# Norms of the first attention by one-pass products of two-part squares, with Newton steps on VectorE

## The chip, the cores and the metric

One core of a Trainium2 chip runs one launch of one program. The metric is the device time of that launch in microseconds, the median of several runs. TensorE does matrix products and transposes into PSUM, VectorE and ScalarE do elementwise work, GpSimd some small work, and SyncE issues most transfers. The engines run in order and meet only at semaphores.

## The reference

Two blocks on x of 512 tokens by 1024. The first is a state-space mixer, a gated feed-forward, a differential attention and a second feed-forward; the second is an mLSTM beside a sparse attention. The change touches the attention of the first block alone:

```python
def rms_norm(x, g):
    return x * rsqrt(mean(x * x, axis=-1) + 1e-6) * g

k = rms_norm(k.reshape(s, 8, 2, 64), k_norm_g)       # 8 heads, two halves of 64
q = rms_norm(q.reshape(s, 8, 2, 64), q_norm_g)
p = softmax(q @ k.T * 64 ** -0.5 + bias, causal)     # one for each half
o = (p[half 0] - lam * p[half 1]) @ v                # 128 wide for each head
o = rms_norm(o, subln_g) * (1 - lam_init)
return o @ out_w
```

## The kernel before

Everything is kept with features on the 128 partitions and the 512 tokens in the free dimension. The large products are made from float32 in three parts: a high part of the weights (ScalarE, L314, float32r) times a high and a low part of the input (L290, L291), and a low part of the weights (VectorE, L325) times the high part (L294). These are one-pass products. Products of plain float32 (scores, transposes, product with v, sums of squares) take two passes. A cell is a 128-row slice of a projection, three one-pass products of 512 columns; a tile is 8 cells (6 or 2 in the output projection).

The first attention works through 8 heads in 3 rounds each; round 0 has query blocks 0 and 1, round 1 block 2, round 2 block 3. I write a round as (h, r). All order is written out by hand in one function for each engine:

- TensorE (`attention_pe`, L671) does, in each round, the 8 cells of a projection tile of the next head (`cells_of`), the scores, then `head_sums(h+1, 0)` in round 0 or `out_sums(h-1)` in round 2, the turn of the previous round's attention (`turn_attn`, L745), the product with v of the round before that (`attn_v`, L756), and in round 1 `head_sums(h+1, 1)`. The last two heads have no new tile to fill rounds with; part of head 7's v tile and the cells of the output projection (`out_cells`) are spread there.
- VectorE (`attention_dve`, L1054) does `combine` of the previous round (L1103 to L1109), `logits` (L1093), the evacuation of the new tile (`evac`, L1066) and the low part of the weights (L325), and the norms' last multiplication (`k_norm` L1074, `q_norm` L1079, `out_norm` L1114).
- ScalarE (`attention_act`, L853) splits the weights, copies the turned attention (`turned`, L906), does the exponentials (`exps`, L898) and the squares (L871), copies and squares a head's output (`head_out`, L913, L914), and starts the inverse roots.

A norm before goes: squares on ScalarE; on TensorE four products that put the squares as the stationary operand and two columns (or one) of ones as the moving one (L699, L767), which gives sums by token in 8 (or 4) columns; mean, Ln and Exp(-0.5 ln) on ScalarE (L875 to L877) on those few columns; one Newton step on GpSimd (`attention_pool`, L1007), which for k and q also spreads the result over 512 columns (L1023); four transposes on TensorE (L709, L717) that turn it to features by tokens in PSUM; and the last multiplication on VectorE.

Of the kernel before, what the change touches and what calls it, by code (L numbers as in the profile page):

```python
# [13 lines left out]
T = 512  # L14
P = 128
# [70 lines left out]
def three_parts(nc, A, out):  # L86
    ctx = ExitStack()
    with ctx:
# [14 lines left out]
        SQ = sb("squares", [P, 2, T])  # L103
        ACC = sb("square_sums", [P, T])
# [12 lines left out]
        CV = sb("conv_rows", [P, 2, T])  # L117
        EMB = sb("floor", [P, T])
        RDB = sb("reciprocals", [P, T])
# [493 lines left out]
        MEAN, LOGS, ROOT, NEWT = ([at(NT, 2) for _ in range(2)] for _ in range(4))  # L613
        INV = [buf.rearrange("p (c d) -> p c d", d=P) for buf in (EMB, RDB)]
        OMEAN, OLOG, OROOT, ONEWT, ORMS = (at(NT) for _ in range(5))
# [9 lines left out]
        hsq = sem("head_squares_ready")  # L625
        hss = sem("head_square_sum_done")
# [3 lines left out]
        newton_step = sem("newton_step")  # L630
        inv_ready = sem("head_inv_rms_ready")
        oroot_ready = sem("out_inv_rms_first_ready")
        ro_ready = sem("out_inv_rms_ready")
        kb_done = sem("k_inv_rms_spread")
        qb_done = sem("q_inv_rms_spread")
        qn_ready = sem("head_q_ready")
        outb_done = sem("out_inv_rms_spread")
# [33 lines left out]
        def attention_pe(pe):  # L671
# [16 lines left out]
            def head_sums(h, which):  # L688

                pe.wait_ge(hsq, 2 * h + which + 1)  # L690
                if which == 0 and h >= 1:
                    pe.wait_ge(v_ready, h)
                if which == 1 and h >= 3:
                    pe.wait_ge(oh_ready, h - 2)
                if which == 1 and h >= 1:
                    pe.wait_ge(qn_ready, h)
                for c in range(NT):
                    at = 8 * which + 2 * c
                    mm = nc.tensor.matmul(BANK[6 + which][:, at:at + 2], SQ[:, which, c * P:(c + 1) * P],  # L699
                                          const("half_ones")[:, 0:P:64], start=True, stop=True)  # L700
                mm.then_inc(hss, 1)

            def spread_norm(h, which):

                pe.wait_ge(inv_ready, 2 * h + which + 1)
                if which == 1 and h >= 2:
                    pe.wait_ge(oroot_ready, h - 1)
                for c in range(NT):
                    mm = nc.tensor.transpose(BANK[6 + which][:, c * P:(c + 1) * P],  # L709
                                             INV[which][:, c, :], IDENT)  # L710
# [2161 lines left out]
```

## Time and profile before

| | |
|---|---|
| median of 3 runs | 2050.57 us (2049.69 to 2050.99) |
| span of the profiled execution | 2047.5 us |
| first attention | from about 763 to 1035 us of the span |
| one steady head | 27.33 us |

The profiled execution is known by its span alone; the timed runs are about 3 us longer. In a timeline a row is a start, a length, engine, line, operation, tile names and how many instructions were merged; an idle time before it stands in brackets with what ended it. Lengths of neighbouring products overlap, so their cost is read from start to start. The rows the prediction uses stand below.

### The profile page before, as it was taken

How to read it: one execution, taken by the hardware profiler on the slowest of the kernel's cores; microseconds unless marked ns; L12 is line 12 of the kernel's file. 1: busy time of each engine (PE TensorE's matmuls, PEld its weight loads, DVE VectorE, ACT ScalarE, POOL GpSimd, SP SyncE). 2: the span in 40 equal slices, each digit the busy share in tenths (PEclk: the TensorE clock that was granted, in tenths of full speed). 3: DMA queues.
4: the chain of work that ended last, by engine and by line, in shares of the span. 5: the costliest groups of instructions: out<-in, count | busy, mean ns of one | idle time of the engine just before them, and what ended most of it. 6: DMA issues, size and time to landing. Idle time of an engine off the chain costs nothing.

```text
span 2047.5 us, 26858 instructions
## 1 busy us (share of the span) xinstructions
PE 2026.5 (99%) x10268; PEld 1635.1 (80%) x10268; DVE 1424.9 (70%) x2093; ACT 927.6 (45%) x1601; POOL 63.3 (3%) x132
## 2 busy tenths in 40 slices
PE   9999999999999999999999999999999999999998
PEld 7887878788888887787778888888777777777787
DVE  7788898777775446566577777447877867566664
ACT  5577775344443234455454444224443332444531
POOL 0000001000000001222000000000000000000000
PEclk9999999999999999999999999999999999999999
DMA  5322222233232333111132332333222224111132
GB/s 177 121 73 73 72 82 63 93 96 100 92 102 81 99 108 114 52 62 38 56 112 94 94 101 83 101 99 104 83 83 77 78 82 165 53 52 52 52 103 83
DMA packets 56225, 179.46 MB, mean 88 GB/s; under 512 B 6287, under 2 KB 9487, under 8 KB 55992
## 3 DMA queue, kind: packets, MB, share of 16 engines
q1 hardware_dynamic: 52416, 167.80, 26.2%
q10 hardware_dynamic: 3704, 10.30, 1.5%
q8 instruction: 61, 1.00, 0.2%
q14 instruction: 44, 0.36, 0.1%
HBM read 175.95 MB, written 4.74 MB: 88 GB/s over the span
## 4 chain that ended last, share of the span: by engine, by line
PE 50%; DVE 1%; ACT 1%; DMA 0%; issue 0%; DVEq 0%
PE bankpair L290 14%; PE bankpair L294 14%; PE bankpair L291 14%; PE bankpair L1532 1%; PE bankpair L1564 1%; PE bankpair L1544 1%; PE bankpair L1400 1%; PE bankpair L1388 1%; PE bankpair L1476 0%; PE bankpair L526 0%; PE bankpair L1457 0%; DMA weight_ring<-up_dram 0%; PE bankpair L1407 0%; DVE residual L2191 0%; PE bankpair L1560 0%; ACT L1726 0%
## 5 line engine op out<-in xcount | busy, mean ns | idle before, releaser
L290 PE MATMUL bankpair<-scaled_in_high,weights_high 128*128 128x512 f32 x1856 | 743.8, 401 | 1.8 <-DVE scaled_in_low L999 0.7
L291 PE MATMUL bankpair<-scaled_in_low,weights_high 128*128 128x512 f32 x1856 | 723.5, 390 | 0.0
L314 ACT ACTIVATE weights_high<-weight_ring 128x1024 fp32r<-128x1024 f32 (+3 forms) x344 | 334.0, 972 | 339.7 <-DMA weight_ring<-down_dram 148.6
L294 PE MATMUL bankpair<-scaled_in_high,weights_low 128*128 128x512 f32 x1856 | 463.0, 389 | 0.0
L325 DVE TENSOR_TENSOR weights_low<-weight_ring,weights_high 128x1024 fp32r<-128x1024 f32 (+3 forms) x344 | 384.1, 1125 | 57.4 <-ACT weights_high L314 47.8
L290 PEld LDWEIGHTS bankpair<-scaled_in_high,weights_high 128*128 128x128 f32 x1856 | 348.7, 188 | 83.0 <-issue 6.5
L291 PEld LDWEIGHTS bankpair<-scaled_in_low,weights_high 128*128 128x128 f32 x1856 | 348.8, 188 | 75.5 <-issue 5.7
L294 PEld LDWEIGHTS bankpair<-scaled_in_high,weights_low 128*128 128x128 f32 x1856 | 348.4, 188 | 72.5
L290 PE MATMUL bankpair<-gated_high,weights_high 128*128 128x512 f32 x448 | 175.1, 391 | 1.9 <-DVE gated_low L2629 1.2
L291 PE MATMUL bankpair<-gated_low,weights_high 128*128 128x512 f32 x384 | 149.4, 389 | 0.0
L589 DVE SCALAR_TENSOR_TENSOR conv_rows<-padded_rows,params,conv_rows 128x512 f32<-128x512 f32 x176 | 131.8, 749 | 7.0 <-ACT conv_rows L558 3.8
L583 DVE TENSOR_TENSOR padded_rows<-bankpair,inv_rms 128x512 f32<-128x512 f32 x88 | 60.9, 691 | 106.4 <-PE bankpair L294 106.1
L558 ACT ACTIVATE conv_rows<-padded_rows,params 128x512 f32<-128x512 f32 x88 | 71.9, 817 | 121.3 <-DVE padded_rows L583 120.8
L294 PE MATMUL bankpair<-gated_high,weights_low 128*128 128x512 f32 x448 | 115.2, 389 | 0.0
L290 PEld LDWEIGHTS bankpair<-gated_high,weights_high 128*128 128x128 f32 x448 | 84.1, 188 | 21.2 <-DVE gated_low L2629 2.5
L294 PEld LDWEIGHTS bankpair<-gated_high,weights_low 128*128 128x128 f32 x448 | 84.1, 188 | 17.5
L500 DVE TENSOR_TENSOR residual<-residual,bankpair 128x512 f32<-128x512 f32 x24 | 16.5, 687 | 98.9 <-PE bankpair L294 98.7
L291 PEld LDWEIGHTS bankpair<-gated_low,weights_high 128*128 128x128 f32 x384 | 72.1, 188 | 14.8
L1093 DVE CUSTOM_DVE_ANT_0 arena<-bankpair,arena 128x128 f32<-128x128 f32 (+3 forms) x64 | 31.4, 491 | 61.2 <-PE bankpair L735 59.7
L1886 DVE TENSOR_TENSOR padded_rows<-bankpair,inv_rms 128x512 f32<-128x512 f32 x44 | 30.4, 690 | 48.4 <-PE bankpair L294 47.2
L566 ACT ACTIVATE gated_high<-conv_rows 128x512 fp32r<-128x512 f32 x44 | 27.8, 632 | 73.3 <-DVE conv_rows L594 73.3
L563 ACT ACTIVATE arena<-conv_rows 128x512 f32<-128x512 f32 x44 | 27.8, 633 | 70.8 <-DVE conv_rows L589 70.8
(396 smaller groups left out, 2396.4 us busy)
## 6 DMA issues: line engine op xcount, KB each, us to landing
weight_ring<-up_dram SPq DMA_DIRECT2D x88, 512.0 KB, 3.5
weight_ring<-w_in_dram SPq DMA_DIRECT2D x70, 512.0 KB, 3.5
weight_ring<-in_w_dram SPq DMA_DIRECT2D x40, 512.0 KB, 3.6
weight_ring<-down_dram SPq DMA_DIRECT2D x32, 384.0 KB, 3.1
weight_ring<-kvq_dram SPq DMA_DIRECT2D x24, 512.0 KB, 3.5
weight_ring<-down_dram SPq DMA_DIRECT2D x32, 320.0 KB, 2.8
weight_ring<-out_a_dram SPq DMA_DIRECT2D x8, 512.0 KB, 3.6
weight_ring<-out_b_dram SPq DMA_DIRECT2D x8, 512.0 KB, 3.6
```

Source lines behind the costliest of these rows:

```text
L290: nc.tensor.matmul(bank, WH[:, high_slot, cell], high, start=(k == 0), stop=False)
L291: nc.tensor.matmul(bank, WH[:, high_slot, cell], low, start=False, stop=False)
L294: mm = nc.tensor.matmul(bank, WL[:, slot, cell], high, start=False, stop=(c == last_k))
L314: nc.scalar.activation(WH[:, (PART0[name] + k) % SLOTS, 0:n], RAW[:, b % SLOTS, 0:n], ACT.Copy).then_inc(high_ready, 1)
L325: nc.vector.tensor_tensor(WL[:, b % SLOTS, 0:n], RAW[:, b % SLOTS, 0:n], WH[:, (PART0[name] + k) % SLOTS, 0:n].bitcast(F32), ALU.subtract) ...
L558: nc.scalar.activation(CV[:, b, :], U[:, b, 3:3 + T], ACT.Identity, bias=par(f"ffn_conv{layer}", 4 * n + 3), scale=par(f"ffn_conv{layer}", ...
L563: nc.scalar.activation(GATE, CV[:, 0, :], ACT.Silu).then_inc(row_used, 1)
L566: nc.scalar.activation(FFH[:, m, :], CV[:, 1, :], ACT.Copy).then_inc(gated_high, 1)
L583: fr.step(nc.vector.tensor_tensor(U[:, b, 3:3 + T], gemm_bank(name, n), RS[:, :], ALU.mult))
L589: (step if b or k == 0 else cv).step(nc.vector.scalar_tensor_tensor(CV[:, b, :], U[:, b, 1 + k:1 + k + T], par(f"ffn_conv{layer}", 4 * n + ...
L1093: (lr if last else step).step(nc.vector.tensor_tensor_reduce(PR[w % 2][c][:, at:at + n], BANK[2 + c][:, at:at + n], BIAS[:, h, T - n:T], - ...
L1886: fr.step(nc.vector.tensor_tensor(dst, gemm_bank(W2, n), RS[:, :], ALU.mult))
```

## The change

The norms become: high part of the squares (ScalarE, float32r) and the whole squares (ScalarE), low part (VectorE); on TensorE two accumulating one-pass products of 512 columns with a full 128 by 128 matrix of ones (or of two 64 by 64 blocks of ones) as the stationary operand, so that the sum already stands on every partition; Ln and Exp on ScalarE on 512 columns; one Newton step as three scalar_tensor_tensor on VectorE on 512 columns; and the last multiplication, which now reads SBUF. GpSimd has no part left in it, and the transposes `spread_norm` and `spread_out` are gone. The two matrices of ones are copied to float32r by ScalarE at the start of the attention. Lines with no content but "..." stand for what is left out.

```diff
@@ TensorE
             def head_sums(h, which):
-                pe.wait_ge(hsq, 2 * h + which + 1)
+                pe.wait_ge(hsl, 2 * h + which + 1)
                 if which == 0 and h >= 1:
                     pe.wait_ge(v_ready, h)
+                if which == 1 and h >= 1:
+                    pe.wait_ge(hs_read[1], h)
                 if which == 1 and h >= 3:
-                    pe.wait_ge(oh_ready, h - 2)
-                if which == 1 and h >= 1:
-                    pe.wait_ge(qn_ready, h)
-                for c in range(NT):
-                    at = 8 * which + 2 * c
-                    mm = nc.tensor.matmul(BANK[6 + which][:, at:at + 2], SQ[:, which, c * P:(c + 1) * P],
-                                          const("half_ones")[:, 0:P:64], start=True, stop=True)
-                mm.then_inc(hss, 1)
-            def spread_norm(h, which):
...
-            def spread_out(h):
...
+                    pe.wait_ge(os_read, h - 2)
+                nc.tensor.matmul(BANK[6 + which][:, :], HALF_R, ROOT_R[which], start=True, stop=False)
+                nc.tensor.matmul(BANK[6 + which][:, :], HALF_R, SQ_R[:, which, :], start=False,
+                                 stop=True).then_inc(hss, 1)
             def out_sums(h):
...
+                pe.wait_ge(osl, h + 1)
+                pe.wait_ge(hs_read[1], min(h + 3, AH))
                 if h >= 1:
-                    pe.wait_ge(oh_ready, h)
-                for c in range(NT):
-                    mm = nc.tensor.matmul(BANK[7][:, c:c + 1], SQO[:, c * P:(c + 1) * P], ONES[:, 0:1], start=True, stop=True)
-                mm.then_inc(oss_done, 1)
+                    pe.wait_ge(os_read, h)
+                nc.tensor.matmul(BANK[7][:, :], ONES_R, OUT_R[:, :], start=True, stop=False)
+                nc.tensor.matmul(BANK[7][:, :], ONES_R, ACC_R[:, :], start=False, stop=True).then_inc(oss_done, 1)
...
-            out_cells(33, 36)
+            out_cells(33, 38)
             out_sums(AH - 1)
-            out_cells(36, 42)
-            spread_out(AH - 1)
-            out_cells(42, 48)
+            out_cells(38, 48)
@@ ScalarE
+            act.wait_ge(gemm_done, TILE0["down0"] + KD)
+            nc.scalar.activation(ONES_R, ONES[:, :], ACT.Copy).then_inc(ones_r, 1)
+            nc.scalar.activation(HALF_R, const("half_ones"), ACT.Copy).then_inc(ones_r, 1)
...
-                nc.scalar.activation(SQ[:, which, :], U[:, 0, 3:3 + T] if which == 0 else QN[h % 2],
-                                     ACT.Square).then_inc(hsq, 1)
+                    act.wait_ge((kq_ready, qn_ready)[which], h)
+                raw = U[:, 0, 3:3 + T] if which == 0 else QN[h % 2]
+                nc.scalar.activation(ROOT_R[which], raw, ACT.Square).then_inc(hsq, 1)
+                nc.scalar.activation(SQ[:, which, :], raw, ACT.Square).then_inc(hsq, 1)
...
+            def first_root(root, sums, scale):
+                logs.step(nc.scalar.activation(root, sums, ACT.Ln, bias=EPSC[:, 0:1], scale=scale))
+                return nc.scalar.activation(root, root, ACT.Exp, scale=-0.5)
...
                 nc.scalar.activation(OB, BANK[5][:, :], ACT.Copy).then_inc(ob_ready, 1)
+                nc.scalar.activation(OUT_R[:, :], BANK[5][:, :], ACT.Square).then_inc(ob_ready, 1)
                 nc.scalar.activation(SQO, BANK[5][:, :], ACT.Square).then_inc(ob_ready, 1)
...
                     exps(h, r)
                     if r == 0 and h + 1 < AH:
+                        inverse(h + 1, 0)
                         squares(h + 1, 1)
-                        inverse(h + 1, 0)
@@ GpSimd
-        def attention_pool(pool):
...
@@ VectorE
+            def low_squares(h, which):
+                dve.wait_ge(hsq, 2 * (2 * h + which + 1))
+                sq = SQ[:, which, :]
+                nc.vector.tensor_tensor(SQ_R[:, which, :], sq, ROOT_R[which].bitcast(F32), ALU.subtract).then_inc(hsl, 1)
+            def low_out_squares(h):
+                dve.wait_ge(ob_ready, 3 * h + 3)
+                nc.vector.tensor_tensor(ACC_R[:, :], SQO, OUT_R[:, :].bitcast(F32), ALU.subtract).then_inc(osl, 1)
+            def newton(root, sums, n, read):
+                read.step(nc.vector.scalar_tensor_tensor(NEWT, sums, n * EPS, root, ALU.add, ALU.mult))
+                step.step(nc.vector.scalar_tensor_tensor(NEWT, NEWT, -0.5 / n, root, ALU.mult, ALU.mult))
+                step.step(nc.vector.scalar_tensor_tensor(root, NEWT, 1.5, root, ALU.add, ALU.mult))
+            def head_root(h, which):
+                dve.wait_ge(root_ready, 2 * h + which + 1)
+                newton(ROOT[which], BANK[6 + which][:, :], 64, hr_read[which])
+            def out_root(h):
+                dve.wait_ge(oroot_ready, h + 1)
+                newton(OROOT, BANK[7][:, :], P, or_read)
...
             evac(0, 1)
+            low_squares(0, 0)
             evac(0, 2)
+            head_root(0, 0)
             k_norm(0)
+            low_squares(0, 1)
             for h in range(AH):
                 for r in range(NR):
                     w = NR * h + r
                     if w == 0:
                         evac(1, 0)
+                        low_squares(1, 0)
+                    if r == 0 and 1 <= h < AH - 1:
+                        low_squares(h + 1, 0)
                     if r == 0:
+                        if h == 0:
+                            head_root(0, 1)
                         q_norm(h)
                     if w >= 1:
                         combine((w - 1) // NR, (w - 1) % NR)
-                    if r == 2 and h + 1 < AH:
+                    if r >= 1 and h + 1 < AH:
+                        head_root(h + 1, r - 1)
+                    if r == 1 and h + 1 < AH:
                         k_norm(h + 1)
+                        low_squares(h + 1, 1)
+                    if r == 2 and h >= 1:
+                        low_out_squares(h - 1)
+                    if r == 0 and h >= 2:
+                        out_root(h - 2)
                     logits(h, r)
...
+            out_root(AH - 2)
             out_norm(AH - 2)
             low_out(AH - 2)
+            low_out_squares(AH - 1)
...
             add_part("attn_a", 6)
+            out_root(AH - 1)
             out_norm(AH - 1)
             low_out(AH - 1)
```

## Rows read from the trace of the kernel before

**Rows 1.** The page's busy times: engine, busy us, share of the span, instructions.
```profile
PE 2026.5 (99%) x10268; PEld 1635.1 (80%) x10268; DVE 1424.9 (70%) x2093; ACT 927.6 (45%) x1601; POOL 63.3 (3%) x132
```

**Rows 2.** Busy time by stretches: a steady head, head 6, then head 7's last round onward.
```profile
869.04:896.37 27.33, 27.33 (x159) 21.98 (x158) 16.52 (x39) 13.11 (x36) 5.61 (x12) 1.00 0.19 58
951.04:967.75 16.71, 14.83 (x101) 11.64 (x101) 13.16 (x35) 11.94 (x36) 4.99 (x12) 1.00 0.08 24
...
984.10:1007.00 22.90, 22.90 (x125) 19.08 (x125) 12.97 (x24) 11.00 (x27) 0.80 (x4) 1.00 0.16 55
```

**Rows 3.** Timeline of TensorE in rounds 0 and 1 of a steady head.
```profile
869.89 1.05 PE L699 MATMUL bankpair<-constants,squares 128*128 128x2 f32 x8
870.81 0.63 PE L745 MATMUL bankpair<-constants,arena 128*128 128x128 f32 x4
...
871.95 0.60 PE L717 MATMUL bankpair<-constants,arena 128*128 128x128 f32 x4
872.30 0.47 PE L290 MATMUL bankpair<-scaled_in_high,weights_high 128*128 128x512 f32 x1
872.62 0.39 PE L291 MATMUL bankpair<-scaled_in_low,weights_high 128*128 128x512 f32 x1
...
877.95 0.92 PE L735 MATMUL bankpair<-arena 64*128 64x384 f32 x4
```

**Rows 4.** Timeline of VectorE over one steady head.
```profile
860.86 0.69 DVE L1093 CUSTOM_DVE_ANT_0 arena<-bankpair,arena 128x512 f32<-128x512 f32 x1 [3.37 <-PE bankpair L735]
...
862.33 0.69 DVE L1066 TENSOR_TENSOR padded_rows<-bankpair,inv_rms 128x512 f32<-128x512 f32 x1
...
864.20 0.68 DVE L1079 TENSOR_TENSOR arena<-arena,bankpair 128x512 f32<-128x512 f32 x1
...
865.83 0.75 DVE L1109 SCALAR_TENSOR_TENSOR arena<-arena 128x512 f32<-128x512 f32 x1
870.11 0.29 DVE L1093 CUSTOM_DVE_ANT_0 arena<-bankpair,arena 128x128 f32<-128x128 f32 x1 [3.53 <-PE bankpair L735]
...
879.00 0.56 DVE L1093 CUSTOM_DVE_ANT_0 arena<-bankpair,arena 128x384 f32<-128x384 f32 x1 [2.62 <-PE bankpair L735]
...
882.58 0.17 DVE L1103 RECIPROCAL arena<-arena 128x2 f32<-128x2 f32 x1 [0.42 <-ACT arena L898]
```

**Rows 5.** Timeline of ScalarE in round 2 of a steady head.
```profile
861.74 0.26 ACT L875 ACTIVATE arena<-bankpair,eps_column 128x4 f32<-128x4 f32 x1 [4.94 <-PE bankpair L767]
...
862.38 0.47 ACT L906 ACTIVATE arena<-bankpair 128x384 f32<-128x384 f32 x1
862.75 0.72 ACT L898 ACTIVATE arena<-arena 128x512 f32<-128x512 f32 x1
...
864.17 0.62 ACT L871 ACTIVATE squares<-padded_rows 128x512 f32<-128x512 f32 x1
```

**Rows 6.** Timeline of VectorE: logits (5,2), (6,2), (7,0), then combine (7,1).
```profile
942.86 0.69 DVE L1093 CUSTOM_DVE_ANT_0 arena<-bankpair,arena 128x512 f32<-128x512 f32 x1 [3.36 <-PE bankpair L735]
...
964.19 0.69 DVE L1093 CUSTOM_DVE_ANT_0 arena<-bankpair,arena 128x512 f32<-128x512 f32 x1
...
969.36 0.29 DVE L1093 CUSTOM_DVE_ANT_0 arena<-bankpair,arena 128x128 f32<-128x128 f32 x1
...
985.87 0.17 DVE L1103 RECIPROCAL arena<-arena 128x2 f32<-128x2 f32 x1 [2.83 <-ACT arena L898]
```

**Rows 7.** Timelines of TensorE and of VectorE at the attention's start.
```profile
773.71 0.95 PE L699 MATMUL bankpair<-constants,squares 128*128 128x2 f32 x8
...
790.76 0.93 PE L735 MATMUL bankpair<-arena 64*128 64x128 f32 x8
...
766.58 3.35 DVE L366 RECIPROCAL inv_rms<-rms 128x512 f32<-128x512 f32 x1 [0.31 <-ACT rms L357]
...
775.11 0.69 DVE L1066 TENSOR_TENSOR padded_rows<-bankpair,inv_rms 128x512 f32<-128x512 f32 x1
```

**Rows 8.** Timeline of TensorE: the sum of head 6's output squares.
```profile
985.15 1.05 PE L767 MATMUL bankpair<-ones,square_sums 128*128 128x1 f32 x8
```

More of the change, by code:

```diff
@@ L102, in three_parts @@
         WL = sb("weights_low", [P, SLOTS, CELLS * P], F32R)
-        SQ = sb("squares", [P, 2, T])
-        ACC = sb("square_sums", [P, T])
+        ONES_R = sb("ones_for_parts", [P, P], F32R)[:, :]
+        HALF_R = sb("half_ones_for_parts", [P, P], F32R)[:, :]
+        with ExitStack() as whole_squares:
+            SQ = whole_squares.enter_context(nc.sbuf_tensor("squares", [P, 2, T], F32))
+            ACC = whole_squares.enter_context(nc.sbuf_tensor("square_sums", [P, T], F32))
+        SQ_R = sb("squares_low", [P, 2, T], F32R)
+        ACC_R = sb("out_squares_low", [P, T], F32R)
         RS = sb("inv_rms", [P, T])
@@ L612, in three_parts @@
         SUMS = [at(4) for _ in range(2)]
-        MEAN, LOGS, ROOT, NEWT = ([at(NT, 2) for _ in range(2)] for _ in range(4))
-        INV = [buf.rearrange("p (c d) -> p c d", d=P) for buf in (EMB, RDB)]
-        OMEAN, OLOG, OROOT, ONEWT, ORMS = (at(NT) for _ in range(5))
+        ROOT = [CV[:, 0, :], CV[:, 1, :]]
+        OROOT = RDB[:, :]
+        NEWT = EMB[:, :]
+        ROOT_R = [HIGH_R[:, 0, :], HIGH_R[:, 1, :]]
         LAM = at(72)
@@ L824, in attention_pe @@
                             head_sums(h + 1, 1)
[L825 to L831 removed]
+                        if r == 2 and h < AH - 2:
+                            turn_v(h + 1)
                     if (h, r) == (AH - 1, 0):
@@ L870, in squares @@
                     act.wait_ge(hss, 2 * h + which - 1)
-                nc.scalar.activation(SQ[:, which, :], U[:, 0, 3:3 + T] if which == 0 else QN[h % 2],
-                                     ACT.Square).then_inc(hsq, 1)
-            def first_root(mean, log, root, sums, scale):
-                logs.step(nc.scalar.activation(mean, sums, ACT.Identity, bias=EPSC[:, 0:1], scale=scale))
-                logs.step(nc.scalar.activation(log, mean, ACT.Ln))
-                return nc.scalar.activation(root, log, ACT.Exp, scale=-0.5)
+                    act.wait_ge((kq_ready, qn_ready)[which], h)
[5 more added lines that the diff above has]
+                return nc.scalar.activation(root, root, ACT.Exp, scale=-0.5)
             def inverse(h, which):
                 act.wait_ge(hss, 2 * h + which + 1)
-                if h >= 1:
-                    act.wait_ge(inv_ready, 2 * h + which - 1)
-                sums = BANK[6 + which][:, 8 * which:8 * which + 8].rearrange("p (c n) -> p c n", n=2)
-                first_root(MEAN[which], LOGS[which], ROOT[which], sums, 1.0 / 64).then_inc(root_ready, 1)
+                first_root(ROOT[which], BANK[6 + which][:, :], 1.0 / 64).then_inc(root_ready, 1)
             def v_out(h):
@@ L1056, in attention_dve @@
             qn = Count(dve, qn_ready)
+            hr_read, or_read = [Count(dve, s) for s in hs_read], Count(dve, os_read)
             def evac(h, j):
@@ L1112, in out_norm @@
             def out_norm(h):
-                dve.wait_ge(outb_done, h + 1)
-                ohr.step(nc.vector.scalar_tensor_tensor(OH[:, h, :], OB, LAM[:, 69:70], BANK[7][:, :], ALU.mult, ALU.mult))
+                ohr.step(nc.vector.scalar_tensor_tensor(OH[:, h, :], OB, LAM[:, 69:70], OROOT, ALU.mult, ALU.mult))
             def add_part(name, j):
```

88 lines of the change are left out of this document (16 added, 72 removed).

## The prediction

> **What bounds the kernel now.** First the page's busy shares [rows 1]: TensorE is busy 99% of the span, so the program is a chain of TensorE work. Then busy time by stretches [rows 2]: in a steady head of the first attention (27.33 us) TensorE is busy throughout, VectorE 16.5, ScalarE 13.1 and GpSimd 5.6 us, at a granted clock of 1.00. From head 6 on this changes: little projection work is left to fill the rounds, and in the 16.71 us of head 6 TensorE is busy 14.83 and VectorE 13.16 us. Then the timelines of TensorE, VectorE and ScalarE over one steady head [rows 3 to 5], which give the prices, and VectorE's in heads 5 to 7 [rows 6].
>
> I call a round (h, r). TensorE is in order: cells of the projection, scores, sums, the turn of the round before, its product with v. VectorE is in order too: combine of the round before, logits, evacuation, weight split. Its gaps in a steady head are the bracketed 3.37, 3.53, 2.62 and 0.42 us of [rows 4]: 9.9 us free, 17.4 us occupied.
>
> **TensorE's part.** Start to start, a sum of squares costs 0.92 us (869.89 to 870.81) and a spread of four transposes 0.35 (871.95 to 872.30) [rows 3]. A steady head has three of each: 3.8 us are removed. Added are three pairs of one-pass products of 512 columns. 24 such passes take 5.65 us (872.30 to 877.95), 0.235 each, and the first after two-pass work 0.32, so 0.09 for the change of kind [rows 3]. A pair costs between 0.46 and, if it is no cheaper than what it replaces, 0.92 us; I take 0.55, near the passes' own row: 1.65 a head. TensorE alone would need 27.33 - 3.8 + 1.65 = 25.2 us.
>
> **VectorE's part.** Per head three low parts (a tensor_tensor on 512 columns, 0.68 us by L1079, 0.62 start to start where nothing waits) and three Newton passes of three scalar_tensor_tensor each. One is 0.75 us on 512 columns of SBUF, 0.78 with the wait for itself [rows 4]; with a PSUM operand I take the same, as L1079, which has one, is no dearer than its kind. A pass costs 2.34. Sum 3 x 0.62 + 3 x 2.34 = 8.9 us, so VectorE is occupied 17.4 + 8.9 = 26.3 us: more than TensorE's 25.2. The bound passes to VectorE. GpSimd's 5.6 us vanish; nobody waited for long on them.
>
> **ScalarE's part.** A square is 0.62 us, 0.52 start to start; there are three more. Each root becomes Ln and Exp on 512 columns. No row shows that Ln: it lies between the square's 0.62 and the 0.72 of an Exp with bias and running sum [rows 5]. I take 0.64 + 0.62 + 0.03 = 1.3 us to the result, where three small activations took 0.64 (861.74 to 862.38). ScalarE's total, 13.1 + 3 x 0.52 + 3 x 0.6 = 16.5 us, is no bound, but its order matters. In (h, 2) it does out_inverse, turned, exps, then both squares of the next k. out_inverse waits for out_sums, and that for low_out_squares, which VectorE makes just ahead of the same round's logits. Counted from the start of logits(h, 2): product done at 0.95, Ln and Exp to 2.2, turned 0.37, exps 1.42, two squares 1.14: 5.1. VectorE, after logits 1.47, evacuation and split 1.87 [rows 4], reaches low_squares(h+2, 0) at 3.3. It waits 1.8 us, or 1.5 where out_sums begins with the end of the scores.
>
> **A second wait, on TensorE.** In (h, 1) head_sums(h+1, 1) stands ahead of the next round's cells and needs low_squares(h+1, 1), which VectorE ends 2.34 + 0.77 + 0.62 = 3.7 us after the combine that releases turn_attn; TensorE has 1.3 us of work there. It idles some 2.3 us.
>
> **The steady head after.** From logits(h, 2) = 0, low_squares(h+2, 0) starts at 4.8. Then 0.62, q_norm 0.71, combine 1.70, out_root 2.34, logits 1.60, evacuation and split 1.87, out_norm 0.77, combine 2.02, Newton 2.34, k_norm 0.77, low part 0.62: 15.4 on, at 20.2, low_squares(h+2, 1) is done. TensorE then does the pair with its release (0.8), eight cells (5.65) and the scores up to the next logits (1.28): 27.9. VectorE's own way is 27.7. A head takes 27.9 us against 27.33: +0.55, four times (heads 1 to 5): +2.2.
>
> **Before that.** TensorE summed the first squares at 773.71 [rows 7]; now it waits for evac(0, 1), which starts at 775.11, and a low part, to 776.5: 2.8 us. The second sum waits until VectorE is through evac(0, 2), Newton and k_norm. Counted through with the same prices, the first scores start at 794.4 instead of 790.76 [rows 7]: +3.7. Heads 0 and 1 have the (h, 1) wait too, against the sums and spreads saved: +0.4. At logits(5, 2) the lag is 3.7 + 0.4 + 2.2 = 6.3 us.
>
> **Heads 6 and 7 carry the loss,** as TensorE has no cells there that would cover it. From logits(5, 2) to logits(6, 2) it was 964.19 - 942.86 = 21.3 us [rows 6]. Now: the wait to 4.8, then the steps above to the split of (6, 1), 17.2; exps 0.4, combine 1.50, Newton 2.34, low part 0.62: 26.9, so +5.5. From there to logits(7, 0) it was 5.2 us [rows 6]; now out_inverse, turned and exps put the combine at 4.75, then 1.70 and out_root(5) 2.34: 8.8, so +3.6. The lag is 15.4, and the chain low_out, evac, out_norm(5), high_out, low_out(5), scores(7, 1) carries it over unchanged. In (7, 2) out_sums(6) started at 985.15 [rows 8]; with the lag TensorE gets there at 1000.6. Now it waits until VectorE, after the exps, has combined (7, 1) and made the low part. That combine started at 985.87 [rows 6]: 985.87 + 15.4 + 0.49 (one more square ahead on ScalarE) + 1.50 + 0.62 = 1003.9, so +3.3. Lag 18.7. From there TensorE is busy to the end [rows 2], so the lag is carried, less two spreads and a cheaper sum (-1.1), plus about 1.4 for out_sums(7), moved back two cells but behind low_out_squares(7), and for the last Newton pass ahead of attn_b. **End: +19 us.** The sum stands against the profiled 2047.5 us; the timed runs (median 2050.57) have some 3 us around the span, which the change leaves. 2050.6 + 19 = **2069.5 us**, 0.9% slower.
>
> At nothing I cost the two copies that make the one-pass ones: 2 x 0.3 us on ScalarE ahead of high_query, under VectorE's 3.35 us reciprocal [rows 7]; without that cover, 0.6. The same for inverse moved ahead of squares(h+1, 1): VectorE's combine, 2.02 us, covers the root's 1.3.
>
> **Rivals.** (1) The steady heads lose nothing: the waits of 1.5 and 2.3 us fall into slack that I misjudge, a head takes VectorE's bare 26.3 us (-1.0, five times), and heads 6 and 7 lose 2 less. For it: the two waits hang on orders with little margin. Against: the durations alone give head 6 most of its +5.5 and +3.6. Time: 2069.5 - 2.2 - 5 - 2 = 2060; chance 0.18.
> (2) Faster: TensorE stays the bound in every head, 8 x (3.8 - 1.65) = -17 us, 2033. One mechanism: VectorE's additions fit its free time. It decides if a Newton step costs under 0.78 - (26.3 - 25.2)/9 = 0.66 us, and head 6, where VectorE has 3.6 us free of 16.7 [rows 2], still loses. The 0.75 us of the nearest row speaks against it. Chance 0.08. Between it and (1), within 0.2% (4 us, about what a measurement of this kernel can tell from no change): 0.07.
> (3) TensorE's clock. It stays at 1.00 in every stretch read, though TensorE is idle for 1.9 of the 16.71 us of head 6 [rows 2]. After, I expect idle spells of 4.7 us at out_sums(5), 4.1 at the first out_cells, 3.3 at out_sums(6). If the clock then falls to 1.2 GHz, steps of 0.235 become 0.47 for a while. The first two falls lie under VectorE's lateness, the third does not; it is bounded by nothing and by the seven cells behind it at half speed (5 us): up to +5, 2074. Chance 0.12.
> The Trainium skill ("TensorE: Matmul & The Clock Gate", Part 1) has the clock at 1.2 GHz after an idle spell until work has been sustained again; by that rule (3) is what happens and 2074 the time. No row here has a spell long enough to say.
> My own forecast: 0.55.
>
> **How the numbers follow.** The likeliest case is 2069.5; its own range, from Newton steps 5% cheaper and a pair at 0.46 (-5) to a pair at 0.92, Ln at 0.72 and dearer releases (+5), is 2064 to 2075. For 8 in 10 it reaches down past (1) with some spread of its own and up past (3): 2056 to 2076. Slower by over 0.2%: 0.55 + 0.18 + 0.12 = 0.85; same 0.07; faster 0.08.
>
> **What the profile after would show.** 72 new scalar_tensor_tensor on the roots at 0.75 us; once a head VectorE waiting 1.5 us ahead of low_squares for ScalarE's squares; TensorE idle 2.3 us in each (h, 1) ahead of the pair, and 3 to 5 us at out_sums(5) and out_sums(6), released by VectorE; scores of a steady head 27.9 us apart; logits(6, 0) some 6 us late, scores(7, 1) 15, attn_b 19, and nothing changed after it. I am wrong if steady heads are shorter than 27.3, or if VectorE has more room in heads 6 and 7 than its gaps tell.

## The result, and the profile after

| | before | after |
|---|---|---|
| median of the timed runs | 2050.13 us (2049.16 to 2050.99, 4 runs) | 2076.36 us (2074.18 to 2076.5, 4 runs) |
| profiled execution, its span | 2047.5 us | 2072.0 us |

The ratio is 1.0129, with a 95% interval of 1.0117 to 1.0141: slower by 1.3%. The forecast was 2069.5 us with a range up to 2076; the time lies 0.4 us above it. The sign is as forecast, and so is the path through VectorE; the size is 7 us too small, for a term that the sum put at nothing.

The page's busy times, against [rows 1]: VectorE gained 66 us, GpSimd lost 42, and TensorE's share fell from 99% to 97%.

```profile
PE 2020.0 (97%) x10028; PEld 1620.3 (78%) x10028; DVE 1490.5 (72%) x2189; ACT 956.4 (46%) x1603; POOL 21.2 (1%) x36
```

Busy time by stretches, against [rows 2]: a steady head from scores to scores, head 6, and 36 us from just ahead of out_sums(6) (not the same work as the last row there). The columns are stretch, length, then busy time of PE, PEld, DVE, ACT and POOL, granted clock, DMA share, GB/s.

```profile
893.23:920.75 27.52, 25.21 (x129) 19.24 (x128) 24.62 (x52) 16.77 (x36) 0.00 (x0) 1.00 0.19 58
957.04:981.84 24.80, 16.59 (x72) 11.22 (x71) 20.93 (x46) 14.27 (x33) 0.00 (x0) 0.72 0.06 17
1005.00:1041.00 36.00, 32.11 (x141) 26.13 (x142) 21.36 (x36) 12.01 (x23) 0.00 (x0) 0.91 0.13 37
```

TensorE's 27.33 busy of 27.33 us has become 25.21 of 27.52, and VectorE's 16.52 has become 24.62. Head 6 took 16.71 us and takes 24.80. And the granted clock, 1.00 in all three stretches of [rows 2], is 0.72 in head 6.

The timeline of VectorE in a steady head, against [rows 4]: the one idle spell that it has left there, and one Newton pass.

```profile
893.69 0.69 DVE L1019 TENSOR_TENSOR out_squares_low<-square_sums,out_squares_high 128x512 fp32r<-128x512 f32 x1
...
899.42 0.69 DVE L1015 TENSOR_TENSOR squares_low<-squares,squares_high 128x512 fp32r<-128x512 f32 x1 [1.60 <-ACT squares L853]
...
902.45 0.69 DVE L1023 SCALAR_TENSOR_TENSOR floor<-bankpair,reciprocals 128x512 f32<-128x512 f32 x1
903.17 0.69 DVE L1024 SCALAR_TENSOR_TENSOR floor<-floor,reciprocals 128x512 f32<-128x512 f32 x1
903.90 0.69 DVE L1025 SCALAR_TENSOR_TENSOR reciprocals<-floor,reciprocals 128x512 f32<-128x512 f32 x1
```

Four gaps of 9.9 us in all have become one of 1.60; the forecast said 1.5, at this place and behind this instruction of ScalarE. A Newton step takes 0.69 us and comes every 0.72 to 0.73, where the forecast had 0.78.

The timeline of ScalarE in round 2, against [rows 5]: Ln and Exp on 512 columns stand where three small activations stood, and the squares of the next k are two.

```profile
895.21 0.69 ACT L856 ACTIVATE reciprocals<-bankpair,eps_column 128x512 f32<-128x512 f32 x1 [3.56 <-PE bankpair L755]
895.92 0.63 ACT L857 ACTIVATE reciprocals<-reciprocals 128x512 f32<-128x512 f32 x1
...
898.24 0.62 ACT L852 ACTIVATE squares_high<-padded_rows 128x512 fp32r<-128x512 f32 x1
898.76 0.62 ACT L853 ACTIVATE squares<-padded_rows 128x512 f32<-128x512 f32 x1
```

The timeline of TensorE, against [rows 3], [rows 7] and [rows 8]: the first pair of the attention, the first scores, a pair in round 1 of a steady head, a pair in round 2, and the out sums of heads 5 and 6 with the passes behind them.

```profile
776.88 0.67 PE L705 MATMUL bankpair<-squares_high,half_ones_for_parts 128*128 128x512 f32 x1 [2.79 <-DVE squares_low L1015]
...
795.65 0.93 PE L724 MATMUL bankpair<-arena 64*128 64x128 f32 x8
...
887.09 0.50 PE L705 MATMUL bankpair<-squares_high,half_ones_for_parts 128*128 128x512 f32 x1 [2.22 <-DVE squares_low L1015]
...
894.43 0.50 PE L754 MATMUL bankpair<-out_squares_high,ones_for_parts 128*128 128x512 f32 x1
894.77 0.39 PE L755 MATMUL bankpair<-out_squares_low,ones_for_parts 128*128 128x512 f32 x1
...
976.21 0.79 PE L754 MATMUL bankpair<-out_squares_high,ones_for_parts 128*128 128x512 f32 x1 [3.60 <-DVE out_squares_low L1019]
976.80 0.63 PE L755 MATMUL bankpair<-out_squares_low,ones_for_parts 128*128 128x512 f32 x1
977.23 0.63 PE L298 MATMUL bankpair<-scaled_in_high,weights_high 128*128 128x512 f32 x1
977.65 0.63 PE L299 MATMUL bankpair<-scaled_in_low,weights_high 128*128 128x512 f32 x1
...
1006.92 0.80 PE L754 MATMUL bankpair<-out_squares_high,ones_for_parts 128*128 128x512 f32 x1 [3.38 <-DVE out_squares_low L1019]
```

The waits are where the forecast put them: 2.79 us (2.8 said), 2.22 (2.3 said), 3.38 (3.3 said); the one at out_sums(5) is shorter, 3.60 (4.7 said), and so is the one at the first out_cells, 3.65 at 988.95 (4.1 said). The new thing is behind them. At 977.23 the next pass starts 0.42 us later, where [rows 3] has 0.235. The windows of TensorE over the places with waits show it as granted clock (columns: stretch, length, busy, clock, DMA share, GB/s):

```profile
774.00:778.00 4.00, 1.21 (x4) 0.87 0.98 365
778.00:782.00 4.00, 4.00 (x14) 0.70 0.39 148
...
858.90:862.50 3.60, 3.60 (x10) 0.53 0.00 0
970.00:980.00 10.00, 6.40 (x16) 0.50 0.01 2
1004.00:1012.00 8.00, 5.08 (x12) 0.60 0.01 3
```

0.50 is 1.2 GHz, one of the clock's two levels. VectorE's timeline at logits (5, 2), (6, 2), combine (6, 2), logits (7, 0) and combine (7, 1) answers [rows 6]:

```profile
949.45 0.69 DVE L1057 CUSTOM_DVE_ANT_0 arena<-bankpair,arena 128x512 f32<-128x512 f32 x1
...
976.07 0.68 DVE L1057 CUSTOM_DVE_ANT_0 arena<-bankpair,arena 128x512 f32<-128x512 f32 x1
...
982.66 0.17 DVE L1067 RECIPROCAL arena<-arena 128x2 f32<-128x2 f32 x1 [3.18 <-ACT arena L875]
...
986.54 0.29 DVE L1057 CUSTOM_DVE_ANT_0 arena<-bankpair,arena 128x128 f32<-128x128 f32 x1
...
1004.67 0.17 DVE L1067 RECIPROCAL arena<-arena 128x2 f32<-128x2 f32 x1 [3.32 <-ACT arena L875]
```

How late each place is, in us (the last column is the first experiment's):

| place | before | lag forecast | after | lag | lag with the clock kept up |
|---|---|---|---|---|---|
| first scores; logits (0, 0) | 790.76; 791.88 | 3.7 | 795.65; 796.77 | 4.9 | 3.3 |
| logits (5, 2) | 942.86 | 6.3 | 949.45 | 6.6 | 3.7 |
| logits (6, 2) | 964.19 | 11.8 | 976.07 | 11.9 | 9.0 |
| logits (7, 0) | 969.36 | 15.4 | 986.54 | 17.2 | 12.4 |
| out_sums(6) | 985.15 | 18.7 | 1006.92 | 21.8 | 15.9 |
| end of the span | 2047.5 | 19 | 2072.0 | 24.5 | 16.3 |

The four largest waits of TensorE by what it waited for (in us total, times, longest), all in the attention but for 0.8 us of the third, which lies just behind it:

```profile
PE bankpair L705 <- DVE squares_low L1015: 17.4, 8, 2.8
PE bankpair L754 <- DVE out_squares_low L1019: 8.2, 3, 3.6
PE bankpair L298 <- DVE query_in_low L1086: 4.4, 2, 3.6
PE bankpair L734 <- DVE arena L1073: 2.4, 1, 2.4
```

All are waits for VectorE: 32 us of idle TensorE, against 3.6 in the attention of before. What the change saves on TensorE (17 us by the forecast's prices) stands against them, and the slow clock on top.

### The profile page after: what moved, and what is told of

It reads as the page before. It is cut to its first block, busy times and chain, and to the rows that moved or that the text cites. A ratio compares the mean times of both kernels' runs of the same rounds, so it can differ in the third digit from the quotient of the medians.

```text
span 2072.0 us, 26325 instructions
## 1 busy us (share of the span) xinstructions
PE 2020.0 (97%) x10028; PEld 1620.3 (78%) x10028; DVE 1490.5 (72%) x2189; ACT 956.4 (46%) x1603; POOL 21.2 (1%) x36
## 4 chain that ended last, share of the span: by engine, by line
PE 49%; DVE 2%; ACT 1%; issue 0%; DMA 0%; DVEq 0%; ACTq 0%
PE bankpair L298 14%; PE bankpair L302 14%; PE bankpair L299 14%; PE bankpair L1513 1%; PE bankpair L1545 1%; PE bankpair L1525 1%; PE bankpair L1369 1%; PE bankpair L1381 1%; PE bankpair L1457 0%; PE bankpair L1438 0%; PE bankpair L534 0%; PE bankpair L1388 0%; DVE residual L2172 0%; DMA weight_ring<-up_dram 0%; PE bankpair L1541 0%
## 5 line engine op out<-in xcount | busy, mean ns | idle before, releaser
L298 PE MATMUL bankpair<-query_in_high,weights_high 128*128 128x512 f32 x128 | 56.1, 438 | 5.1 <-DVE query_in_low L1086 4.4
```

The costliest lines, as they stand in the source:

```text
L298: nc.tensor.matmul(bank, WH[:, high_slot, cell], high, start=(k == 0), stop=False)
```

## The experiments

My theory, A: the loss is VectorE's occupied time (in steady heads), then its chain in heads 6 and 7, and on top of it the clock that falls behind TensorE's waits. Each run below was timed beside the kernel before, 2049.1 us in the medians of them all. The kernel after was timed apart from them, beside a before of 2050.1 us, so differences to its median hold to about 1 us; differences of spans compare one profiled execution with another. The times of the steady head are from logits (4, 2) to logits (5, 2).

**1. Products in the waits.** One-pass products of 512 columns into a bank that nobody reads are put ahead of the waiting instructions; nothing else is changed.

```diff
+            def busy(n, turned_before):
+                if turned_before > 0:
+                    pe.wait_ge(t_ready, turned_before)
+                for _ in range(n):
+                    nc.tensor.matmul(BANK[4][:, :], HALF_R, HH[:, 0, :], start=True, stop=True)
...
+            busy(10, 0)
             head_sums(0, 0)
```

> Adds idle work only: in each of TensorE's waits of the attention (two at its start, one in round 1 of each head but head 1, those at turn_attn(6, 0), out_sums(5), the third cell of the output projection, out_sums(6)) TensorE first does 5 to 15 one-pass products of 512 columns whose result nobody reads, fewer than the wait is long. They shorten nothing; they only keep TensorE busy. Theory A (some of the loss is TensorE's clock, which falls to half during the waits and stays there for up to 3.5 us of work behind them): granted clock back at 1.00, no product of 512 columns at 0.43 us, and the kernel is 5 to 7 us faster than the changed one: 2069 to 2072 us. Theory B (the slow stretches lie under VectorE's lateness and cost nothing): within 1.5 us of 2076.4, or a little slower where a product overhangs its wait.

Measured: 2065.96 us (2065.46 to 2066.36), ratio 1.0082 (1.0068 to 1.0096): 10.4 us less than after (9.6 by the two ratios), span 8.2 less. Theory A, with more to gain than its 5 to 7 us. The windows of TensorE, the same places:

```profile
960.00:970.00 10.00, 8.69 (x42) 1.00 0.00 1
970.00:980.00 10.00, 8.70 (x46) 1.00 0.01 2
980.00:990.00 10.00, 8.80 (x45) 1.00 0.14 39
```

The clock stays at 2.4 GHz, and the lags of the last column of the table come out. By differences the clock had cost 1.6 us at the start, some 1.5 in head 2, 2.0 from logits (6, 2) to (7, 0), 1.1 to out_sums(6), and 2.3 behind it (each to 0.1 or 0.2 us). The steady head is 27.55 us, unchanged: the clock has no part in it.

**2. Newton on one column.** The three steps run on one column of 512, so the other columns keep the first root of Ln and Exp.

```diff
-                read.step(nc.vector.scalar_tensor_tensor(NEWT, sums, ...
...
+                root, sums, t = root[:, 0:1], sums[:, 0:1], NEWT[:, 0:1]
+                read.step(nc.vector.scalar_tensor_tensor(t, sums, ...
...
```

> The Newton step is done on one column of the 512 alone, so the other columns of each norm keep the first root of Ln and Exp: part of the computation is left out. VectorE's three instructions fall from 2.17 us to about 0.5 us, 24 times. Theory A (VectorE's added work is the bound): a steady head falls from 27.5 us to TensorE's own 25.2 to 25.8 us, heads 6 and 7 lose little, total about 2040 us (2034 to 2048), faster than before the change. Theory B (the bound is elsewhere, in ScalarE's longer roots and squares or in the order of the waits): 2060 us or more.

Measured: 2049.42 us (2047.38 to 2050.65), ratio 1.0000 (0.9991 to 1.0009), 27 us less than after, just above theory A's 2034 to 2048. Its steady head:

```profile
909.29:934.15 24.86, 24.86 (x129) 19.17 (x130) 19.91 (x51) 16.65 (x36) 0.00 (x0) 1.00 0.18 58
```

TensorE is busy for all of it again. So the new work of TensorE does fit in 24.9 us (25.2 forecast), 2.5 less than before the change; nothing but VectorE's Newton steps keeps the steady head above that. That this kernel is no faster than before all the same is due to the start and heads 6 and 7, where the low parts and the waits for them stay: against before, the first logits are 3.5 us late, logits (5, 2) 8.7 us early (934.15), and the end of the span 1.0 us late. The clock falls in heads 6 and 7 there too (0.80 granted from 960 to 970), so these 9.7 us are waits and clock together.

**3. The low part of the next k behind combine.** It took the place of VectorE's 1.60 us of idle time.

```diff
-                    if r == 0 and 1 <= h < AH - 1:
-                        low_squares(h + 1, 0)
                     ...
                         combine((w - 1) // NR, (w - 1) % NR)
+                    if r == 0 and 1 <= h < AH - 1:
+                        low_squares(h + 1, 0)
```

> In round 0 VectorE makes the low part of the next head's k squares behind q_norm and combine, not ahead of them. Theory A (VectorE is saturated in a steady head, 25.9 us of work and 1.6 us of waiting for ScalarE's squares): the wait goes and a steady head falls from 27.5 to 26.0 to 26.4 us, four to five times: 2076.4 - 6 = 2070 us (2068 to 2072). Theory B (TensorE's wait of 2.2 us in round 1 closes the loop, with VectorE's wait only slack): no change within 1.5 us.

Measured: 2065.15 us (2063.32 to 2066.69), ratio 1.0076 (1.0063 to 1.0090), 11 us less than after, and below theory A's 2068 to 2072. Its steady head is shorter by 1.5 us, about the idle spell; the spans differ by 7.5 us: the first logits come 1.8 us later than after (798.57 against 796.77), and from logits (1, 2) to (6, 2) 9.1 us are gained, the fall of the clock in head 2 among them, which is missing here. What makes the medians differ by more is not shown; the execution profiled here was the longest of its five.

```profile
917.55:943.55 26.00, 25.21 (x128) 19.24 (x128) 24.53 (x52) 16.78 (x36) 0.00 (x0) 1.00 0.18 56
```

**4. The low part of the head's output.** Behind combine in heads 1 to 6 it stands ahead of Newton and k_norm; in head 7 it goes ahead of combine.

```diff
+                    if (h, r) == (AH - 1, 2):
+                        low_out_squares(h - 1)
                     if w >= 1:
                         combine((w - 1) // NR, (w - 1) % NR)
+                    if r == 2 and 1 <= h < AH - 1:
+                        low_out_squares(h - 1)
...
-                    if r == 2 and h >= 1:
-                        low_out_squares(h - 1)
```

> In round 2 VectorE makes the low part of the output's squares ahead of the Newton step, and in (7, 2) ahead of combine, so that out_sums is released 2.2 us (head 5) and about 2.9 us (head 6) earlier; steady heads have no wait there and do not change. Theory A (out_sums(6)'s wait is paid in full, since TensorE is the bound behind it, out_sums(5)'s only in part): 3 us less for the first, with the slow clock behind it up to 2 more: 2071 to 2074 us. Theory B (VectorE's total decides heads 6 and 7, so the order does not matter): within 1.5 us of 2076.4.

Measured: 2065.94 us (2065.75 to 2067.57), ratio 1.0084 (1.0070 to 1.0097), 10 us less than after (6.6 in the spans), more than theory A said. The steady head is 27.4 us, as after. The gain lies in heads 6 and 7: logits (7, 0) at 984.58 against 986.54, (7, 2) at 1005.08 against 1006.79, and 4.9 us from there to the end of the span: the out sums of head 6 wait 0.70 us there instead of 3.38, and the granted clock from 1000 to 1020 us is 1.00 (0.83 after).

**5. The q pair between cells.** TensorE's wait of 2.2 us in (h, 1) is taken away by itself.

```diff
+                    elif r == 2 and h + 1 < AH:
+                        cells_of(h + 2, 0, 3)
+                        head_sums(h + 1, 1)
+                        cells_of(h + 2, 3, 8)
...
-                        if r == 1:
-                            head_sums(h + 1, 1)
```

> One part alone: the pair of products for the next q is no longer put ahead of the cells of round (h, 2) but between the third and the fourth of them, so that TensorE does not wait for VectorE's low part in (h, 1). Theory A (VectorE is the bound of a steady head; its only idle time there is the 1.6 us ahead of the low part of the next k): TensorE's wait of 2.2 us disappears from its row, comes back at the next thing that VectorE makes for it, and the steady head stays at 27.3 to 27.5 us; in all -1 to -4 us, what there is coming from clock falls that do not happen: 2072 to 2075. Rival B (my forecast's own chain of the steady head, in which that wait stands on the path): 2.2 us less in each of heads 0 to 6, -13 to -15 us, 2062.

Measured: 2069.64 us (2069.12 to 2071.9), ratio 1.0104 (1.0088 to 1.0119), 6.7 us less than after. Theory A's steady head holds and rival B's falls: 27.53 us, although the wait at L705 is gone. It came back at the out sums:

```profile
PE bankpair L754 <- DVE out_squares_low L1021: 18.1, 8, 4.5
PE bankpair L705 <- DVE squares_low L1017: 7.1, 6, 2.8
```

The total gained more than theory A's 1 to 4 us. Logits (2, 2) stand at 861.90 against 867.03, 5.1 us earlier, and the gain is carried from there. 1.8 us of it are there at logits (0, 0) already, where this kernel does nothing else than the one after: its first pair waits 2.80 us too, but the clock does not fall behind it. The rest comes in heads 0 to 2, and the fall in head 2 (some 1.5 us) is part of it.

**6. Two Newton steps on GpSimd.** From head 1 on VectorE does the first step, which reads the sums; GpSimd does the rest as three instructions. To give it time, k_norm moves to the next round, and the Newton pass of the outputs to the start of its round.

```diff
+            for which, h in ON_POOL:
+                root, n = (*ROOT, OROOT)[which], (64, 64, P)[which]
+                pool.wait_ge((hs_read[0], hs_read[1], os_read)[which], h + 1)
+                st.step(nc.gpsimd.tensor_tensor(NEWT, NEWT, root, ALU.mult))
+                st.step(nc.gpsimd.tensor_scalar(NEWT, NEWT, -0.5 / n, 1.5, ALU.mult, ALU.add))
+                st.step(nc.gpsimd.tensor_tensor(root, NEWT, root, ALU.mult))
```

> Of every Newton pass from head 1 on (for the heads' outputs up to head 5) VectorE does the first step alone, which reads the sums; the other two go to GpSimd as three instructions on 512 columns (1.04 to 1.16 us each by GpSimd's own 512-column rows before the change), and the norm that uses the root stands a round or half a round later. Theory A (VectorE's occupied time is what the change costs in steady heads): it loses 6 steps of 0.72 us a head, 27.5 - 1.6 - 4.3 = 21.6, so TensorE is the bound again and the steady head is that of the one-column run, 24.9 us; the time comes near that run's 2049.4: 2046 to 2053. Rival B: the root now comes 3.4 us later, so VectorE waits for GpSimd at k_norm or q_norm and takes back 1 to 3 us a head: 2055 to 2066. Rival C: GpSimd and VectorE slow each other in the same memory, VectorE's steps of 0.69 us become dearer while GpSimd works: steady head over 26 us, 2055 or more.

Measured: 2061.02 us (2059.44 to 2062.87), ratio 1.0060 (1.0046 to 1.0073). The steady head is 25.98 us, not 24.9. Rival B's waits are not there: VectorE never waits for GpSimd in that head, its only idle time is 1.18 us ahead of the low part of k, for ScalarE. What it does is longer, as rival C says. The timelines of GpSimd and then of VectorE in it:

```profile
906.70 1.30 POOL L641 TENSOR_TENSOR conv_rows<-floor,conv_rows 128x512 f32<-128x512 f32 x1
911.33 1.76 POOL L639 TENSOR_TENSOR floor<-floor,conv_rows 128x512 f32<-128x512 f32 x1 [3.33 <-DVE floor L1041]
913.18 0.94 POOL L640 TENSOR_SCALAR floor<-floor 128x512 f32<-128x512 f32 x1
...
906.74 2.34 DVE L333 TENSOR_TENSOR weights_low<-weight_ring,weights_high 128x1024 fp32r<-128x1024 f32 x1
...
911.22 0.75 DVE L1060 SCALAR_TENSOR_TENSOR arena<-padded_rows,arena,conv_rows 128x512 f32<-128x512 f32 x1
912.00 1.64 DVE L1035 TENSOR_TENSOR out_squares_low<-square_sums,out_squares_high 128x512 fp32r<-128x512 f32 x1
913.56 0.68 DVE L1079 CUSTOM_DVE_ANT_0 arena<-bankpair,arena 128x512 f32<-128x512 f32 x1
```

VectorE's split of the weights (1.22 to 1.23 us elsewhere) takes 2.34, and the low part (0.69) 1.64; each ends 1.1 and 0.55 us behind the end of GpSimd's instruction (908.00, 913.09), which is about its own work. The logits at 913.56, which read one operand from PSUM and one from SBUF, are not longer, though GpSimd is at work beside them. The Trainium skill ("GPSIMD Engine Reference", Key points) says that the two engines share their SBUF interfaces, with contention for VectorE instructions that have two SBUF inputs; the trace agrees, by the 1.1 and 0.95 us that such instructions gain here.

**7. The three orders together** (3, 4 and 5 in one kernel; no work taken away).

> No work is taken away or moved to another engine, only three places in the orders: the low part of the next k behind combine, the low part of the head's output behind combine in heads 1 to 6 and ahead of combine in head 7, the q pair between the cells. Theory A (each order removes a wait of its own): the two measured alone gave -11 and -10 us and the third gives some -2, so 2051 to 2056, with a steady head of 25.9 us. Rival B (the gains alone were mostly the same clock falls in heads 6 and 7, and can be had once): 2060 to 2064.

Measured: 2054.97 us (2053.47 to 2055.68), ratio 1.0026 (1.0016 to 1.0036): 21 us less than after. Theory A. The steady head is 25.70 us, with no idle time of VectorE in it: that is VectorE's own way.

**8. GpSimd and orders** (6 with the orders of 4 and 5).

> The kernel with two Newton steps on GpSimd, and in it the order of the out low part and of the q pair. Theory A (what is left beside VectorE's occupied time are the waits at the out sums and in heads 6 and 7): 5 to 10 us below that kernel, 2038 to 2046, which would be faster than the kernel before the change. Rival B: with VectorE no longer full those waits are covered already, and the orders change nothing: within 2 us of the kernel with the steps on GpSimd alone.

Measured: 2054.17 us (2052.86 to 2054.67), ratio 1.0023 (1.0014 to 1.0032). 7 us below the sixth, as theory A said of the step, but 8 us above its number, which had the sixth at 2050. Steady head 25.87 us: GpSimd gives nothing that the orders alone don't.

**9. A Newton pass of two instructions**, in the kernel of 7. ScalarE makes the root's square as well, by one more Exp from the same logarithm; the constants 1/(2n) and the sign go into the gains.

```diff
+                logs.step(nc.scalar.activation(square, root, ACT.Exp, scale=-1.0))
                 return nc.scalar.activation(root, root, ACT.Exp, scale=-0.5)
...
-                read.step(nc.vector.scalar_tensor_tensor(NEWT, sums, n * EPS, root, ALU.add, ALU.mult))
-                step.step(nc.vector.scalar_tensor_tensor(NEWT, NEWT, -0.5 / n, root, ALU.mult, ALU.mult))
-                step.step(nc.vector.scalar_tensor_tensor(root, NEWT, 1.5, root, ALU.add, ALU.mult))
+                read.step(nc.vector.scalar_tensor_tensor(square, sums, n * EPS, square, ALU.add, ALU.mult))
+                step.step(nc.vector.scalar_tensor_tensor(root, square, 3.0 * n, root, ALU.subtract, ALU.mult))
```

> The kernel with the three orders, and in it a Newton pass of two VectorE instructions instead of three: ScalarE makes one Exp more (the root's square, from the same logarithm), and the constants go into the gains. Theory A (VectorE's occupied time): 3 x 0.72 = 2.2 us a head fewer on VectorE, so the steady head falls from 25.7 us to TensorE's own 24.9, and the chain in heads 6 and 7 loses a step in each of two passes; 2045 to 2050 in all, against 2055 with the orders alone. Rival B (the roots' latency counts, not VectorE's time): ScalarE's Exp of 0.63 us more delays every root by as much as VectorE gains on it, and the time stays at 2053 to 2056.

Measured: 2046.77 us (2044.92 to 2049.24), ratio 0.9989 (0.9980 to 0.9998). Theory A. Its steady head:

```profile
910.90:935.76 24.86, 24.86 (x129) 19.18 (x129) 22.35 (x48) 18.55 (x39) 0.00 (x0) 1.00 0.19 58
```

**10. The same with products in the waits that are left.**

> The same as the kernel with the two-step Newton, and one-pass products into an unused bank in the waits of TensorE that are left: 10 and 5 at the start, 7, 7, 7, 12 and 3 in heads 6 and 7. Theory A (the granted clock falls behind each of those waits and what follows runs at half speed): 4 to 8 us less than without them. Rival B (waits are shorter here than in the kernel after the change, so the clock hardly falls): within 2 us.

Measured: 2042.85 us (2042.34 to 2043.24), ratio 0.9968 (0.9956 to 0.9980): 3.9 us less than 9, at the edge of theory A's 4 to 8, and faster than both kernels. In the spans it is 6.3 us (the execution of 9 that was profiled was one of its longer ones), of which 3.3 are there at the first logits already. The windows of TensorE around head 6, of 9 and then of 10:

```profile
950.00:960.00 10.00, 4.84 (x21) 0.87 0.00 0
960.00:970.00 10.00, 7.57 (x33) 0.79 0.13 42
970.00:980.00 10.00, 9.54 (x41) 0.83 0.14 40
...
950.00:960.00 10.00, 7.78 (x42) 1.00 0.00 0
960.00:970.00 10.00, 10.00 (x52) 1.00 0.13 41
970.00:980.00 10.00, 10.00 (x49) 1.00 0.26 80
```

**11. Orders and products, with the full Newton passes** (7 with products in its waits).

> The kernel with the three orders and the full Newton passes, and one-pass products in the waits that it has left (10 and 5 at the start, 8, 8, 8, 14 and 3 in heads 6 and 7). Theory A (clock): it has 0.74, 0.58 and 0.83 granted from 950 to 980 us, half speed for some 8 us, so 4 to 6 us less than the 2055 of the orders alone: 2048 to 2052, level with the kernel before. Rival B: the slow stretches lie under VectorE's lateness, nothing gained: 2054 to 2056.

Measured: 2050.41 us (2050.1 to 2053.12), ratio 1.0008 (0.9998 to 1.0017), 4.6 us less than 7: level with the kernel before.

## Why the prediction was right in kind and short in size

**The bound passes to VectorE: right.** 24.6 us busy and 1.60 idle in a head of 27.52 (the rest are the gaps of some hundredths between its instructions), and its idle spell, not TensorE's, sets the head (experiments 3 and 5). VectorE's own way was forecast at 27.7 us and is 27.5; its occupied time is 25.9 where I had 26.3. The difference is the Newton step, 0.72 to 0.73 us from one to the next where I took 0.78 from the dearer kind of [rows 4]: nine of them make 0.5 us.

**The second wait, TensorE's 2.3 us in (h, 1): there, 2.22 us, and it costs nothing in a steady head.** The forecast's 27.9 us was counted along the path that goes over this wait, 0.2 us above VectorE's own way. Experiment 5 shows that this path does not set the head: without the wait it is 27.53 us still. The wait has a price I did not see: in head 2 the clock fell behind one such wait.

**Heads 6 and 7: right.** With the clock kept up, the lags grow from logits (5, 2) to (6, 2) by 5.3 us (5.5 forecast), to (7, 0) by 3.3 (3.6), to out_sums(6) by 3.5 (3.3), to the end by 0.4 (0.3). These four terms are good to 0.3 us.

**The clock: the step that failed.** The sum put it at nothing. I made it a rival, (3), with a chance of 0.12, priced up to +5 us, by the argument that "the first two falls lie under VectorE's lateness, the third does not". Experiment 1 measures 8.2 us in spans and 10.4 in medians for all falls. Two things were wrong in it. The falls are more: I listed spells of 3.3 us and above, but the clock fell behind the 2.79 us at the start (0.70 granted from 778 to 782) and behind one of the 2.2 us in (h, 1), at 858.10. And the falls in heads 6 and 7 do not lie under VectorE's lateness. By experiment 1 they cost 2.0 us between logits (6, 2) and (7, 0) and 1.1 more to out_sums(6): VectorE's combine of (6, 2) waits 3.18 us there (982.66) for ScalarE's exponentials. These stand behind the copy of the turned attention, which itself waits for TensorE, and TensorE has two cells at half speed to do ahead of that turn (977.23 to 979.79). I had nothing but ScalarE's own order (out_inverse, turned, exps) in the 4.75 us from these logits to the combine; they are 6.6 us, and 4.6 in experiment 1. Only the third, 2.3 us, was counted, at most as 5. The Trainium skill ("TensorE: Matmul & The Clock Gate", Part 1) has the clock at 1.2 GHz after an idle spell; the runs agree for the spells of 3.38 to 3.65 us, with 0.50 granted from 970 to 980, and the chance should have been far above 0.12.

**Sum.** In spans, the chain that I counted gives 16.3 us without the clock, where I had 19: 1.5 of the difference lie in the steady heads, 0.8 in heads 0 and 1, 0.4 at the start. 8.2 us of clock make it 24.5. So the two errors run against each other, and it is luck that the lags at logits (5, 2) and (6, 2), 6.6 and 11.9 us, stand within 0.3 of the forecast: without the clock they are 3.7 and 9.0. In spans the miss of 5.5 us is 8.2 less 2.7. The medians differ by 26.2, mostly because the profiled execution is the shortest of its four: the others have spans of 2074.1 to 2074.3. So a common run of the kernel after, 9.6 to 10.4 us above that of experiment 1, pays some 10 us for the clock; that the last 2 of them are one fall more is likely, not shown.

**The other rivals.** (1), that a steady head falls to 26.3 us, is refuted: it takes 27.52, a little more than the 27.33 of before; (2), that TensorE stays the bound, needed a step under 0.66 us and found 0.72. But its picture of the steady head, TensorE busy throughout in 24.86 us, is what experiments 9 and 10 make true by taking a third of Newton's steps off VectorE.

## What to carry to other kernels

When a change saves on the full engine and adds to another, add up that other engine's occupied time per period first: here VectorE's 25.9 us against TensorE's 24.9, and VectorE's one idle spell, made 0.2 us lost in each steady head out of what could have been 2.5 saved, and a third off one small pass turned a ratio of 1.0026 into 0.9989. Look as well where the full engine has little work to cover a wait: most of the loss lies in the last two heads. Then list the waits that the full engine gets, and price each twice: the wait itself, and the slow clock behind it on every pass up to the next instruction that somebody waits for. Where such a wait can't be removed, useless one-pass products in it paid 4 to 10 us here.

## What the runs showed of the hardware

- Equal waits do not have equal effects: of the spells of 2.22, 2.22, 2.24 and 2.20 us in (2, 1) to (5, 1), only the first, at 858.10, was followed by 1.2 GHz (passes 0.43 us apart from 858.9 to 862.3). The next, 2.25 us in (6, 1), came after 1.4 us of work behind another of 2.36, and there the first pass (969.38) was slow already. And the wait of 2.8 us at the start was followed by 0.70 in the kernel after and by 1.00 in experiment 5. So a forecast can give such a fall a chance and a price, not a place.
- The first pass after an idle spell takes 0.79 to 0.80 us at the slow clock (969.38, 976.21, 988.95, 1006.92), the next ones 0.63, with starts 0.42 to 0.43 apart.
- A scalar_tensor_tensor on 512 columns takes 0.69 us here, also with one operand in PSUM, where combine's and k_norm's take 0.75. What makes the difference wasn't tried.
- A VectorE instruction with two SBUF inputs that starts while one of GpSimd runs ends about its own length behind that, as if it had waited for it, even if it is short: in experiment 6 a tensor_tensor on one column, elsewhere 0.16 us, began at 894.82 and took 0.93, up to the end of a GpSimd product (894.13, 1.60 us long). GpSimd is slowed too: its 512-column tensor_tensor took 1.26 to 2.28 us there, and two of the longer ones, 1.76 at 911.33 and 1.60 at 894.13, began while such an instruction of VectorE was running.
- Transposes of plain float32 do not belong with the products that I called two-pass: in [rows 3] the four of a spread are x4, one record each, where the four products of a sum are x8. The prediction took both from their measured times, so no term hangs on it.
